# Output weights' parts stored once and loaded ready, and the attention's output split where it is copied, in a decoder-layer kernel

## The chip, the cores and the metric

The kernel runs on 1 core of a Trainium2 chip. The metric is device time in microseconds. The kernel before takes 3652.9 us (median of three runs, 3649.78 to 3656.28). The word core always means this one NeuronCore, with its engines TensorE (PE; its weight loads are PEld), VectorE (DVE), ScalarE (ACT), GpSimd (POOL) and SyncE (SP), which here issues nearly all DMAs.

## The reference, cut to what matters

One layer over 2048 prompt tokens and 64 sample tokens, model width 1024. An indexer picks 256 keys per token, eight heads attend to them (attention output `a_o`, 512 wide), and a state-space mixer gives `s_o` (512 wide). What follows is the part that the change touches:

```python
def residual_block(x, a_o, s_o, w_out, g_post, g_ffn_pre, w_up, w_down, g_ffn_post):
    mix = jnp.concatenate([a_o, s_o], axis=-1) @ w_out
    x = x + rmsnorm(mix, g_post)
    hdn = jnp.square(jax.nn.relu(rmsnorm(x, g_ffn_pre) @ w_up))
    return x + rmsnorm(hdn @ w_down, g_ffn_post)
```

## The kernel before, in words

The second half of the kernel (`blend`) starts at about 730 us. It walks a list of units, `plan`, and each engine executes its part of each unit in that one order. Units of three kinds are woven together by costs: the index search (`S`), the attention (`A`) and the feed (`W`, `M`, `N`, `U`, `D`, `E`), which is the residual block. The feed runs over four groups of 512 tokens (group 3 has a fifth tile, the samples). In a group:

- `W, g, h, i` is the output projection of token tile i into half h of the columns: 8 row blocks k of `w_out`, three matmuls each, 24 matmuls. All tiles of h = 0 come first, then all of h = 1.
- `M` is the norm after it and the norm before the MLP, tile by tile on ACT, DVE and POOL; `N` turns the result for the MLP.
- `U, g, j` (32 of them) and `D, g, m, q` (16 times four) are the MLP up and down; `E` is the last norm and the output store, beside the last `D` units and the next group's first `W` units.

Products are taken in three passes on operands split in two: hi (ACT rounds a copy to the reduced 32-bit format) and lo (DVE subtracts hi from the raw value). So a matrix needs one ACT copy and one DVE subtraction per piece before PE can use it. The MLP weights are split once, in group 0, stored to HBM in both parts (`ws_d`, L1343), and loaded ready by groups 1 to 3 into six slots (`load_ready`, L1339). The output weights are not: each group loads all 16 raw pieces (256 KB, L1352), ACT splits them (L1861) and DVE (L2197), into X, which holds one half h only. Half 0 of the next group is split beside the last eight `D` units, two pieces at each of four of them. Half 1 can only be split when the last `W, g, 0` unit has read X, at `W, g, 1, 0`.

The features of a tile are `a_d` (attention) and `so_d` (state space), 256 KB each, loaded by SP (L1365) and split by ACT (L1871) and DVE (L2204). Tiles 0 and 1 lie in region DN, 2 and 3 in H. PE waits for both low halves (L1574).

The attention's output of a tile is turned by PE (L1708) into one of two PSUM banks `tr`, copied by ACT (L1989), and stored by SP (L1463). The other uses of these banks are the turns of the probabilities (L1691), one per head and 512 keys.

SP has one queue of instructions and waits in order; a DMA whose wait is not yet met holds up all that stand behind it. `y_p` (L1428) is the store of the layer's result at `E`, which waits for POOL's last addition, and `m_d` (L1479) is the store of a selection mask, which waits for DVE's search.

## Time and profile before

| | |
|---|---|
| median of the runs | 3652.9 us (3649.78, 3652.9, 3656.28) |
| profiled execution | 3654.93 us, span 3653.3 us, mean granted clock 0.912 |
| PE busy | 3051.2 us, 84% |
| DVE, ACT, POOL busy | 1838.9, 1636.2, 1262.7 us |
| DMA | 529.45 MB, mean 145 GB/s |

Times are microseconds from the span's start, and the profiled execution's own time is its span and 1.6 us around it. PE is the busiest engine. Its longest idle stretches in the feed lie at the turns from one group to the next, at about 965 to 1078, 1623 to 1768, 2328 to 2475 and 3084 to 3209 us. In the rows, `x_hi_b` and `x_lo_b` are X, `dn_b` and `h_b` hold the features (and, elsewhere, `dn_b` down weights), `xs_b` is the raw input of the features, `r` are the three PSUM banks of the feed, `part_b` is where ACT copies a down sum from one of them before POOL adds it (L2111).

### The profile page before, as it was taken

The numbers are of one execution on the slowest core, as the hardware profiler recorded it, in microseconds if no ns is written. First come the engines' busy times: TensorE is split into PE (matmuls) and PEld (weight loads), VectorE is DVE, ScalarE is ACT, GpSimd is POOL, SyncE is SP. The second block draws the span as 40 slices with busy tenths as digits, with TensorE's granted clock in tenths as the row PEclk, the third lists the DMA queues.
The fourth block names the chain that finished last, engine by engine and source line by source line (L and its number), as shares of the span: only waits on it lengthen the run. The fifth ranks groups of instructions, "written<-read, shape, count | busy, mean of one in ns | idle before, by whom it ended". The sixth has DMA issues, their size and how long they took to land.

```text
span 3653.3 us, 46908 instructions
## 1 busy us (share of the span) xinstructions
PE 3051.2 (84%) x15352; PEld 2407.0 (66%) x15352; DVE 1838.9 (50%) x4116; ACT 1636.2 (45%) x2873; POOL 1262.7 (35%) x1181
## 2 busy tenths in 40 slices
PE   7998546557678889997799999869999999799997
PEld 6887432224566668765577886646778888578886
DVE  4333972862357974467785332666772333421112
ACT  3322413612456746575563456746734444322222
POOL 1333621323013551252264114522671112224444
PEclk9999767767889999997899999979999999899999
DMA  4444345636336573353454223343443213544443
GB/s 150 139 145 149 87 129 136 159 117 208 104 138 228 210 244 112 136 215 127 175 186 160 80 72 112 129 177 132 167 174 106 70 61 127 187 149 151 173 150 124
DMA packets 216109, 529.45 MB, mean 145 GB/s; under 512 B 57514, under 2 KB 110828, under 8 KB 189852
## 3 DMA queue, kind: packets, MB, share of 16 engines
q1 hardware_dynamic: 202924, 501.94, 40.4%
q0 software_dynamic: 11360, 22.60, 2.0%
q8 instruction: 125, 2.05, 0.2%
q10 hardware_dynamic: 1584, 1.90, 0.2%
q14 instruction: 116, 0.95, 0.1%
HBM read 399.43 MB, written 134.12 MB: 146 GB/s over the span
## 4 chain that ended last, share of the span: by engine, by line
PE 48%; DVE 12%; issue 11%; ACT 5%; DMA 4%; POOL 4%; SPq 2%; ACTq 0%; POOLq 0%; DVEq 0%
PE r L1620 16%; PE r L1652 12%; PE po L1700 4%; PE tr L1691 3%; ACT junk_a_b L1969 2%; POOL acc_b L2111 1%; PE sc L1679 1%; PE sc L1678 1%; PE r L1809 1%; PE sc L1668 1%; DVE junk_v_b L2350 1%; DVE trial_b L2302 1%; POOL hr_b L2092 1%; PE tr L1668 1%; DVE prob_b L2381 1%
## 5 line engine op out<-in xcount | busy, mean ns | idle before, releaser
L2111 POOL TENSOR_TENSOR acc_b<-acc_b,part_b 128x512 f32<-128x512 f32 x375 | 515.8, 1395 | 494.5 <-ACT part_b L1920 493.6
L1652 PE MATMUL r<-ready_b,h_b 128*128 128x512 f32 x2304 | 565.3, 401 | 44.2 <-ACT part_b L1920 40.2
L1652 PEld LDWEIGHTS r<-ready_b,h_b 128*128 128x128 f32 x2304 | 434.4, 192 | 159.7 <-ACT part_b L1920 52.4
L1620 PE MATMUL r<-x_hi_b,ready_b 128*128 128x512 f32 x1536 | 495.2, 396 | 5.4 <-DVE x_lo_b L2216 2.8
L2092 POOL TENSOR_TENSOR hr_b<-hr_b 128x512 f32<-128x512 f32 x128 | 148.8, 1163 | 780.9 <-ACT hr_b L1907 780.7
L1969 ACT ACTIVATE junk_a_b<-score_b,trial_b 128x384 int8<-128x384 f32 (+13 forms) x266 | 347.5, 1306 | 101.0 <-DVE trial_b L2302 99.9
L1620 PEld LDWEIGHTS r<-x_hi_b,ready_b 128*128 128x128 f32 x1536 | 292.0, 190 | 76.4 <-issue 10.1
L1920 ACT ACTIVATE part_b<-r 128x512 f32<-128x512 f32 x390 | 223.6, 594 | 216.6 <-PE r L1652 127.3
L1620 PE MATMUL r<-x_lo_b,ready_b 128*128 128x512 f32 x768 | 302.0, 393 | 0.0
L1700 PEld LDWEIGHTS po<-V_sb,pT_b 128*128 128x128 f32 x2176 | 286.1, 192 | 23.1 <-issue 3.1
L1996 ACT ACTIVATE pT_b<-tr 128x512 f32<-128x512 f32 (+3 forms) x320 | 168.7, 527 | 264.9 <-PE tr L1691 264.4
L1700 PE MATMUL po<-V_sb,pT_b 128*128 128x64 f32 x2176 | 279.0, 268 | 3.7 <-DVE o_b L2367 3.3
L2381 DVE CUSTOM_DVE_ANT_0 prob_b<-sc,mk_b,mx_b 128x512 f32<-128x512 f32 (+3 forms) x192 | 125.0, 651 | 286.8 <-PE sc L1679 286.4
L2350 DVE TENSOR_SCALAR_CACHE_REDUCE junk_v_b<-score_b,trial_b 128x384 bf16<-128x384 f32 (+13 forms) x182 | 268.2, 1474 | 1.8
L1652 PE MATMUL r<-dn_b,h_b 128*128 128x512 f32 x720 | 188.9, 417 | 42.3 <-ACT part_b L1920 21.0
L2100 POOL TENSOR_TENSOR h_b<-hr_b,h_b 128x512 fp32r<-128x512 f32 x128 | 185.8, 1452 | 96.4 <-ACT h_b L1936 96.4
L2381 DVE CUSTOM_DVE_ANT_0 prob_b<-sc,mk_b 128x512 f32<-128x512 f32 (+3 forms) x128 | 82.1, 642 | 246.3 <-PE sc L1679 177.7
L1691 PE MATMUL tr<-ident_sb,prob_b 128*128 128x128 f32 x1088 | 178.4, 280 | 31.1 <-ACT prob_b L2002 30.2
L1652 PEld LDWEIGHTS r<-dn_b,h_b 128*128 128x128 f32 x720 | 140.2, 200 | 89.3 <-ACT part_b L1920 26.1
L2002 ACT ACTIVATE prob_b<-prob_b,nmx_b 128x128 f32<-128x128 f32 (+15 forms) x128 | 153.9, 1202 | 99.9 <-DVE nmx_b L2387 99.9
L2293 DVE TENSOR_SCALAR turn_b<-count_b 128x1 int32<-128x1 f32 x448 | 68.2, 152 | 249.7 <-ACT junk_a_b L1969 240.4
L1907 ACT ACTIVATE hr_b<-r 128x512 f32<-128x512 f32 x128 | 75.6, 591 | 251.1 <-PE r L1620 251.1
(407 smaller groups left out, 6064.2 us busy)
## 6 DMA issues: line engine op xcount, KB each, us to landing
ready_b<-ws_u SPq DMA_DIRECT2D x96, 1024.0 KB, 6.6
ready_b<-ws_d SPq DMA_DIRECT2D x96, 1024.0 KB, 5.0
ws_u<-up_b SPq DMA_DIRECT2D x32, 1024.0 KB, 9.0
ws_d<-dn_b SPq DMA_DIRECT2D x30, 1024.0 KB, 6.5
kv_b<-kv_pages POOLq DMA_DIRECT2D x128, 128.0 KB, 3.4
kv_b<-kv_pages SPq DMA_DIRECT2D x128, 128.0 KB, 3.1
raw_b<-w_out SPq DMA_DIRECT2D x64, 256.0 KB, 3.4
raw_b<-w_up SPq DMA_DIRECT2D x32, 512.0 KB, 5.5
```

Source lines behind the costliest of these rows:

```text
L1620: mm = pe.matmul(x[:], wt[:, c], y[:, k], start=k == n == 0, stop=(k, n) == (KD - 1, 2))
L1652: mm = pe.matmul(x[:], f[:, tok], w[:, col], start=c == n == 0, stop=(c, n) == (KQ - 1, 2))
L1691: mm = pe.transpose(x[:, (k - 4 * b) * P:(k - 4 * b + 1) * P], prob[:, n % 2, k * P:(k + 1) * P], ident[:])
L1700: mm = pe.matmul(po[:, h, :], pT[:, prob_no[t, h, b] % 3, k - 4 * b, :], R["V"][:, k, n:n + HD], start=k == 0, stop=k == t)
L1920: act.activation(dst, ring[bank_no[key] % RING][:], ACT.Copy).then_inc(free_act, 1)
L1969: act.activation(junk_a[:, 0:width(t)], score[:, n % 3, 0:width(t)], ACT.Sign, bias=trial[:, 0:1].bitcast(F32), accum_out=count[:, 0:1]).t ...
L1996: act.activation(pT[:, j % 3, 0:m, :], tr[i % 2][:, 0:m * P].rearrange("p (k q) -> p k q", q=P), ACT.Copy).then_inc(tr_free, 1)
L2092: pool.tensor_tensor(s, s, s, ALU.mult).then_inc(sq_ok, 1)
L2100: pool.tensor_tensor(z, s, a.bitcast(F32), ALU.subtract).then_inc(h_lo_ok, 1)
L2111: pool.tensor_tensor(dst, dst, part[:, add_no[key] % 2, :], ALU.add).then_inc(add_pool, 1)
L2350: c.step(dve.tensor_scalar(junk_v[:, 0:width(t)], score[:, turn_s[t] % 3, 0:width(t)], trial[:, lower_trial(t)].bitcast(F32), 0.0, ALU.is_ ...
L2381: dve.tensor_tensor_reduce(out=prob[:, n % 2, 512 * b:512 * b + w], in0=sc[i % 2][:, 0:w], in1=mk[:, t % 2, 512 * b:512 * b + w], scale=1. ...
```

## The change

- Group 0 still loads and splits all 16 pieces. SP stores each split piece, both parts, to `wo_d` (16 stores of 512 KB). ACT's first split of half 1 waits for the eight stores of half 0, and its first `N` copy into X for all 16.
- Groups 1 to 3 load and split no raw piece. Half 0 is loaded into X by two DMAs of 2 MB once the previous group's last `U` has run. With it go the first three of eight row blocks of half 1, 1.5 MB in two DMAs, into free slot space (`kept_out`). The other five, 2.5 MB in one DMA, go into X once the last `W, g, 0` unit has run.
- For this slot space the fifth ready MLP piece of a group is loaded at the last `N` unit, beside the sixth, and not beside `W, g, 1, 3`.
- The attention's output is split where it is copied: ACT writes hi (still L1989's copy, now rounding), a new DVE instruction `low_output` writes lo from the same bank, and SP stores both (512 KB). PE waits for the low part before it uses that bank again. `aT` held two tiles; now it holds the two parts of one.
- A tile's attention features are loaded ready into place by one 512 KB DMA (`load_attended`), issued at the unit that uses them and not one tile ahead. Only `so_d` is split, with two input buffers. The sample tile is split as before.

```diff
@@ which parts are split, and where
-            at = [("D", g - 1, ND - 2, 2), ("D", g - 1, ND - 2, 3), ("D", g - 1, ND - 1, 0), ("D", g - 1, ND - 1, 1)]
-            for k in range(8):
-                splits_at[at[k // 2]].append(("wo", g, 0, k))
-        splits_at["W", g, 1, 0] += [("wo", g, 1, k) for k in range(8)]
         if g:
             continue
+        splits_at["W", g, 1, 0] += [("wo", g, 1, k) for k in range(8)]
...
-                where = ("W", g, 1, 3) if n == 4 else ("N", g, nt(g) - 1)
+                where = ("N", g, nt(g) - 1)
@@ memory
+    wo_d = nc.dram_tensor("wo_d", (2, P, 2, KD, 512), F32).ap()
+    a2_d = nc.dram_tensor("a2_d", (NPT, P, 2, 4, P), F32).ap()
+        KEPT = 3
+        kept_out = ready[:, 4:6].rearrange("p s z n -> p (s z) n")[:, 0:KEPT].rearrange("p k (z n) -> p z k n", z=2)
+        def out_weights(g, h, k):
+            if g and h and k < KEPT:
+                return kept_out[:, 0, k], kept_out[:, 1, k]
+            return X[0][:, k], X[1][:, k]
@@ SP
+                def keep_out(x):
+                    sp.wait_ge(lo_ok, split_no[x])
+                    sp.dma_start(wo_d[x[2], :, :, x[3]], x_both[:, :, x[3]].bitcast(F32)).then_inc(wo_st, 16)
+                def load_out(g, h):
+                    if h == 0:
+                        if g == 1:
+                            sp.wait_ge(wo_st, 16 * 16)
+                            sp.wait_ge(lo_ok, split_no["d", 0, NU - 1])
+                        sp.wait_ge(ring_full, all_up(g - 1, NU - 1))
+                        for n, k in enumerate((0, KD // 2)):
+                            sp.dma_start(x_both[:, :, k:k + KD // 2].bitcast(F32), wo_d[0, :, :, k:k + KD // 2]).then_inc(raw_ld[2 * n + 1], 16)
+                        for z in range(2):
+                            sp.dma_start(kept_out[:, z].bitcast(F32), wo_d[1, :, z, 0:KEPT]).then_inc(raw_ld[5], 16)
+                    else:
+                        sp.wait_ge(ring_full, full_at(("W", g, 0, nt(g) - 1)))
+                        sp.dma_start(x_both[:, :, KEPT:KD].bitcast(F32), wo_d[1, :, :, KEPT:KD]).then_inc(raw_ld[7], 16)
...
+                def load_attended(g, i):
+                    t, n = tile0(g) + i, feat_no[g, i]
+                    if i == 4:
+                        return
+                    sp.wait_ge(aT_st[t % 2], 16 * (t // 2 + 1))
...
+                    sp.dma_start(feat_both(i)[:, :, 0:4].bitcast(F32), a2_d[t]).then_inc(fa_ld[n % 2], 16)
...
                     for f, i in feats_at[u]:
+                        load_attended(f, i)
                         if i + 1 < nt(f):
                             load_features(f, i + 1)
+                    if kind == "D" and (u[2], u[3]) == (ND - 2, 2) and g + 1 < NG:
+                        load_out(g + 1, 0)
                     if kind == "W" and u[2:] == (1, 0):
+                        if g:
+                            load_out(g, 1)
@@ TensorE
-                        if i == 0:
+                        if i == 0 and g == 0:
                             pe.wait_ge(lo_ok, split_no["wo", g, h, k])
+                        elif i == 0 and h == 0 and k % 4 == 0:
+                            pe.wait_ge(raw_ld[2 * (k // 4) + 1], 32 + 16 * g)
+                        elif i == 0 and h and k in (0, KEPT):
+                            pe.wait_ge(raw_ld[7 if k else 5], 32 + (16 if k else 32) * g)
...
                     wait(pe, tr_free, n - 1)
+                    if n - 2 in output_at:
+                        pe.wait_ge(aT_lo_ok, output_at[n - 2] + 1)
@@ ScalarE, VectorE: features and the attention's output
-                    for k in range(2):
-                        act.wait_ge(f_ld[k], 16 * (n // 2 + 1))
-                        act.activation(feat(i)[0][:, 4 * k:4 * k + 4], f_in[:, k], ACT.Copy).then_inc(f_hi, 1)
+                    act.wait_ge(f_ld[n % 2], 16 * (n // 2 + 1))
+                    act.activation(feat(i)[0][:, 4:8], f_in[:, n % 2], ACT.Copy).then_inc(f_hi, 1)
...
+                def low_output(t):
+                    n = turn_no["o", t]
+                    dve.wait_ge(tr_free, n + 1)
+                    dve.tensor_tensor(aT[:, 1], tr[n % 2][:].rearrange("p (f q) -> p f q", q=P), aT[:, 0].bitcast(F32),
+                                      ALU.subtract).then_inc(aT_lo_ok, 1)
```

SP's queue at the start of group 0 (`raw_b` is a raw piece, `x_b` is X, `so_d` and `a_d` the two kinds of features, 1024 wide where both parts lie side by side). Before:

```order
L1352 DMA raw_b<-w_out 128x512 [waits y_st]
L1352 DMA raw_b<-w_out 128x512 x7
L1352 DMA raw_b<-w_out 128x512 [waits lo_ok_b] x8
L1365 DMA xs_b<-a_d 128x512 [waits aT_st0__b,h0_ld,bank_full]
L1365 DMA xs_b<-so_d 128x512
```

and after:

```order
L1364 DMA raw_b<-w_out 128x512 [waits y_st]
L1364 DMA raw_b<-w_out 128x512 x7
L1364 DMA raw_b<-w_out 128x512 [waits lo_ok_b] x8
L1343 DMA wo_d<-x_b 256x1x512 [waits lo_ok_b] x8
L1375 DMA xs_b<-so_d 128x512 [waits h0_ld,bank_full]
L1391 DMA dn_b<-a_d 128x2x512 [waits aT_st0__b]
```

Eight stores now stand between the raw loads and the first features.

SP's queue between groups 1 and 2, from the result's stores to the loads for the norm. Before:

```order
L1428 DMA y_p<-acc_b 128x1024 [waits y_ok_b] x4
L1365 DMA xs_b<-a_d 128x512 [waits f_lo_b,aT_st1__b]
L1365 DMA xs_b<-so_d 128x512 [waits f_lo_b]
L1479 DMA m_d<-tie_b 128x1664 [waits mask_ok_b]
L1399 DMA gbuf_b<-g_post 128x1024 [waits yn_ok_b]
L1375 DMA part_b<-x_all 128x1024 [waits add_pool_b]
```

and after:

```order
L1462 DMA y_p<-acc_b 128x1024 [waits y_ok_b] x4
L1391 DMA h_b<-a_d 128x2x512 [waits fa_ld0__b,ring_full_b,aT_st0__b]
L1375 DMA xs_b<-so_d 128x512 [waits f_lo_b]
L1391 DMA h_b<-a_d 128x2x512 [waits fa_ld1__b,ring_full_b,aT_st1__b]
L1513 DMA m_d<-tie_b 128x1664 [waits mask_ok_b]
L1357 DMA x_b<-wo_d 128x2x2560 [waits ring_full_b]
L1432 DMA gbuf_b<-g_post 128x1024 [waits yn_ok_b]
```

The attention features of tile 2 stood ahead of the `y_p` stores and now stand behind them, and the load of half 1's weights stands behind the mask's store.

DVE after the change, in the attention two steps behind a tile's turned output (ISA is the masked maximum over the scores in `sc`):

```order
L2439 ISA prob_b,mx_b<-sc,mk_b,mx_b 128x512 [waits sc_full_b,sc_free_b]
L2439 ISA mx_b 128x1
L2445 TENSOR_SCALAR nmx_b<-mx_b 128x1 [waits sc_free_b]
L2424 TENSOR_TENSOR aT_b<-tr,aT_b 128x512 [waits tr_free_b]
L2439 ISA prob_b,mx_b<-sc,mk_b 128x512 [waits sc_full_b,tr_full_b]
```

The TENSOR_TENSOR between them is new.

## Rows read from the trace of the kernel before

**Rows 1.** Page, busy time by engine.

```profile
PE 3051.2 (84%) x15352; PEld 2407.0 (66%) x15352; DVE 1838.9 (50%) x4116; ACT 1636.2 (45%) x2873; POOL 1262.7 (35%) x1181
```

**Rows 2.** PE, first matmul after its long waits (start, length, [idle <- releaser]).

```profile
984.46 0.80 PE L1586 MATMUL r<-x_hi_b,dn_b 128*128 128x512 f32 x1 [19.02 <-DVE dn_b L2204]
996.41 0.69 PE L1668 MATMUL sc<-kiT_sb,qi_b 64*128 64x512 f32 x1 [3.35 <-DMA qi_b<-qi_d]
1694.43 0.80 PE L1586 MATMUL r<-x_hi_b,h_b 128*128 128x512 f32 x1 [11.33 <-DVE h_b L2204]
1717.37 0.77 PE L1586 MATMUL r<-x_hi_b,dn_b 128*128 128x512 f32 x1 [5.71 <-DVE x_lo_b L2197]
2421.71 0.77 PE L1586 MATMUL r<-x_hi_b,dn_b 128*128 128x512 f32 x1 [9.04 <-DVE x_lo_b L2197]
3125.92 0.79 PE L1586 MATMUL r<-x_hi_b,h_b 128*128 128x512 f32 x1 [8.76 <-DVE h_b L2204]
3136.31 0.50 PE L1586 MATMUL r<-x_hi_b,h_b 128*128 128x512 f32 x1 [2.42 <-DVE h_b L2204]
3151.20 0.76 PE L1586 MATMUL r<-x_hi_b,dn_b 128*128 128x512 f32 x1 [2.02 <-DVE x_lo_b L2197]
```

**Rows 3.** Groups of instructions in 1635 to 1671 us, group 0's last down units.

```profile
L1652 PE MATMUL r<-up_b,h_b 128*128 128x512 f32 x48 | 16.8, 507 | 8.2 <-ACT part_b L1920 8.2
L2197 DVE TENSOR_TENSOR x_lo_b<-raw_b,x_hi_b 128x512 fp32r<-128x512 f32 x8 | 7.3, 955 | 0.4 <-DVE trial_b L2302 0.3
L2204 DVE TENSOR_TENSOR dn_b<-xs_b,dn_b 128x512 fp32r<-128x512 f32 x4 | 5.0, 1283 | 3.4 <-ACT dn_b L1871 3.4
```

**Rows 4.** Groups of instructions in 2331 to 2378 us, group 1's last down units.

```profile
L1652 PE MATMUL r<-ready_b,h_b 128*128 128x512 f32 x87 | 26.8, 462 | 12.0 <-ACT part_b L1920 12.0
L1969 ACT ACTIVATE junk_a_b<-score_b,trial_b 128x1792 int8<-128x1792 f32 x7 | 12.5, 1787 | 7.1 <-DVE trial_b L2302 7.1
L2197 DVE TENSOR_TENSOR x_lo_b<-raw_b,x_hi_b 128x512 fp32r<-128x512 f32 x8 | 8.3, 1089 | 0.1
```

**Rows 5.** Windows: busy us of PE, PEld, DVE, ACT, POOL; granted PE clock, DMA share, GB/s.

```profile
972.00:978.00 6.00, 0.00 (x0) 0.00 (x0) 4.14 (x7) 3.75 (x6) 0.00 (x0) 0.50 0.98 364
1735.00:1747.00 12.00, 6.10 (x27) 4.70 (x26) 6.11 (x15) 6.22 (x14) 3.16 (x2) 0.91 1.00 393
2331.00:2378.00 47.00, 35.02 (x103) 21.51 (x101) 41.82 (x65) 33.70 (x54) 22.31 (x16) 0.84 0.32 100
```

**Rows 6.** SP's queue at four places of the timeline.

```profile
978.07 0.37 SPq L1365 DMA_DIRECT2D xs_b<-a_d  x1
...
1693.85 0.33 SPq L1428 DMA_DIRECT2D y_p<-acc_b  x1
...
2420.87 0.32 SPq L1479 DMA_DIRECT2D m_d<-tie_b  x1
...
3130.44 0.33 SPq L1428 DMA_DIRECT2D y_p<-acc_b  x1
```

**Rows 7.** DMA issues: KB each, us to landing; at 1735.8 us, and at 1694.3 us.

```profile
x_d<-acc_b SPq DMA_DIRECT2D x1, 512.0 KB, 11.7
...
xs_b<-a_d SPq DMA_DIRECT2D x1, 256.0 KB, 3.2
```

**Rows 8.** Timeline, 1747 to 1749 us, group 1's norms.

```profile
1747.57 0.16 DVE L50 RECIPROCAL rs_b<-root_b 128x1 f32<-128x1 f32 x1 [4.38 <-DMA x_d<-acc_b]
...
1748.84 3.19 POOL L2126 TENSOR_TENSOR acc_b<-acc_b,part_b 128x1024 f32<-128x1024 f32 x1 [7.63 <-DMA part_b<-x_all]
```

**Rows 9.** Timeline, 1476 to 1485 us, behind the turned output of tile 6.

```profile
1476.07 0.61 PE L1708 MATMUL tr<-ident_sb,o_b 128*128 128x128 f32 x4
...
1478.26 0.61 PE L1691 MATMUL tr<-ident_sb,prob_b 128*128 128x128 f32 x4
...
1478.52 0.16 DVE L2387 TENSOR_SCALAR nmx_b<-mx_b 128x1 f32<-128x1 f32 x1
...
1481.78 2.99 PE L1652 MATMUL r<-dn_b,h_b 128*128 128x512 f32 x12
```

**Rows 10.** Line L2197 over the span: ns minimum/median/maximum.

```profile
L2197 DVE TENSOR_TENSOR x_lo_b<-raw_b,x_hi_b x64: 679/685/1792, 970.6 to 3154.6; 128x512 fp32r<-128x512 f32 x64
```

More of the change, by code:

```diff
@@ L922, in blend @@
     feats = [x for u in feed for x in feats_at[u]]
-    feat_no = {x: 2 * n for n, x in enumerate(feats)}
+    feat_no = {x: n for n, x in enumerate(feats)}
     def stream(g):
@@ L947, in blend @@
             holder[s] = x
-    for g in range(1, NG):
-        for k in range(8):
-            if g > 1:
-                behind_of["wo", g, 0, k] = 0
-                loads_at["U", g - 1, NU - 1 if k < 4 else NU - 1].append(("wo", g, 0, k))
-        for k in range(8):
-            behind_of["wo", g, 1, k] = split_no["wo", g, 0, k]
-            loads_at[at_split["wo", g, 0, k]].append(("wo", g, 1, k))
     WSLOTS = 6
@@ L1074, in blend @@
     head_at = {n: x for x, n in head_no.items()}
+    output_at = {turn_no["o", t]: t for t in range(NPT)}
     last_bank = lambda n: turn_no["p", *head_at[n], banks(head_at[n][0]) - 1]
@@ L1098, in place_at @@
             return t
-        X = [place_at(f"x_{n}", [P, KD, 512], F32R) for n in ("hi", "lo")]
+        x_both = place_at("x", [P, 2, KD, 512], F32R)
+        X = [x_both[:, n] for n in range(2)]
         H = place_at("h", [P, 8 * 512], F32R)
+        KEPT = 3
         ready = nc.alloc_sbuf_tensor_at("ready_b", [P, WSLOTS, 2, D], F32R, offset=at[0])
@@ L1211, in split_of @@
             if x[0] == "wo":
-                return X[0][:, x[3]], X[1][:, x[3]]
+                return out_weights(0, x[2], x[3])
             return piece(x)
@@ L1217, in split_after @@
             if kind == "wo":
-                if x[2]:
-                    return full_at(("W", g, 0, nt(g) - 1))
-                return all_up(g - 1, NU - 1) if g else 0
+                return full_at(("W", g, 0, nt(g) - 1)) if x[2] else 0
             c = x[2]
@@ L1235, in blend @@
         sring = [*sc, *tr]
-        raw_ld, wo_ld = [sem(f"raw_ld{i}_") for i in range(4)], [sem(f"wo_ld{i}_") for i in range(8)]
+        raw_ld = [sem(f"raw_ld{i}_") for i in range(8)]
         ready_ld = [sem(f"ready_ld{i}_") for i in range(WSLOTS)]
@@ L1355, in load @@
                             sp.wait_ge(xn_ok, last_tile(g))
[L1356 removed]
+                        sp.dma_start(raw_of(x), A["w_up" if kind == "u" else "w_down"][x[2]]).then_inc(raw_ld[2 * slot_of[x]], 16)
                 def load_features(g, i):
[L1359 to L1360 removed]
+                    t, n = tile0(g) + i, feat_no[g, i]
                     if i == 0:
                         wait(sp, res_ok, tile0(g))
[L1363 to L1365 removed]
+                    wait(sp, f_lo, n - 1)
+                    sp.dma_start(f_in[:, n % 2], A["so_d"][t]).then_inc(f_ld[n % 2], 16)
+                    if i == 4:
+                        sp.wait_ge(f_lo, n)
+                        sp.dma_start(f_in[:, 1 - n % 2], A["a_d"][t]).then_inc(f_ld[1 - n % 2], 16)
+                def load_attended(g, i):
+                    t, n = tile0(g) + i, feat_no[g, i]
+                    if i == 4:
+                        return
+                    sp.wait_ge(aT_st[t % 2], 16 * (t // 2 + 1))
+                    if g == 1 and i < 2:
+                        for z in range(2):
+                            sp.wait_ge(kept_st["DN", z], 16 * n_kept["DN", z])
+                    if g:
+                        sp.wait_ge(ring_full, all_down(g - 1, ND - 2 if i < 2 else ND - 1))
+                    wait(sp, fa_ld[n % 2], 16 * (n // 2))
+                    sp.dma_start(feat_both(i)[:, :, 0:4].bitcast(F32), a2_d[t]).then_inc(fa_ld[n % 2], 16)
                 def load_x(g, i):
@@ L1383, in feed_part @@
                     for x in splits_at[u]:
-                        if x[0] != "wo":
+                        if x[0] == "wo":
+                            keep_out(x)
+                        else:
                             keep(x)
@@ L1986, in keep_output @@
                     n = turn_no["o", t]
-                    wait(act, aT_st[t % 2], 16 * (t // 2))
+                    if t:
+                        act.wait_ge(aT_st[(t - 1) % 2], 16 * ((t - 1) // 2 + 1))
                     act.wait_ge(tr_full, n + 1)
-                    act.activation(aT[:, t % 2], tr[n % 2][:].rearrange("p (f q) -> p f q", q=P), ACT.Copy).then_inc(tr_free, 1)
+                    act.activation(aT[:, 0], tr[n % 2][:].rearrange("p (f q) -> p f q", q=P), ACT.Copy).then_inc(tr_free, 1)
                 def keep_prob(t, h, b):
```

71 lines of the change are left out of this document (39 added, 32 removed).

## The prediction

> **What bounds the kernel now.** I read the page first: PE is busy for 84% of the span [rows 1], no other engine for more than half. So the end is PE's stream of instructions, and DVE or ACT time taken away is worth what PE waited for it. Next I looked in PE's timeline for its waits around the output projection, where the removed work sits [rows 2]. There are two kinds: waits for a feature's low part (19.02, 11.33 and 8.76 us) and waits for the low part of half 1's first piece (5.71, 9.04 and 2.02 us). Then I grouped the instructions of the last down units of groups 0 and 1, where half 0 of the next group is split: PE waits there 8.2 and 12.0 us for ACT's copies `part_b` [rows 3, 4], at a mean granted clock of 0.84 in the second [rows 5], and DVE is busy for 41.82 of 47 us with the index search, the splits and the features. ACT's copies stand in its queue behind search counts, which wait for DVE's trial for 7.1 us there [rows 4]. Last I read SP's queue, which decides when the new loads start [rows 6], how long transfers took to land [rows 7], and who waited for them [rows 8]. Sums go against the profiled execution, 3654.9 us, which lies 2.0 above the median of 3652.9; the forecast is given against the median.
>
> **Group 0: 16 stores added.** Eight 512 KB stores, 4.2 MB, enter SP's queue just before the first features, where the load at 978.07 stood [rows 6]. At the 364 GB/s of the stretch before it [rows 5] they take 11.5 us. A 256 KB load landed after 3.2 us [rows 7], of which 0.7 is data at that rate, so 2.5 is fixed; of this I count 2 ahead of the data. The first features then follow at 978.1 + 2 + 11.5 + 0.7 = 992.3, their split (two operations near 0.7 each [rows 10]) ends at 993.7, and PE, which started at 984.46 [rows 2], is 9.2 late. It gets back the 3.35 us that it waited at 996.41 for the search's next load, which stood behind features that each waited for the split before them; with two buffers for `so_d` that load goes out sooner. The other eight stores stand ahead of the weights and tokens of the first norm, whose loads had several us to spare; I take 1.5. Sum +7.4. Bounds: +1 (the stores drain beside the raw loads) and +13 (nothing given back, 4 us at the norm).
>
> **Attention: the low part in front of the bank's next use.** Behind the turned output of tile 6, DVE's maximum and its small follower end at 1478.68; the new instruction takes 0.69 (a 512-wide subtraction [rows 10]) and ends at 1479.4. PE used the bank again at 1478.26 [rows 9]: +1.1 us. Twelve of 16 tiles have such a use soon behind them; where a unit of the feed stands in between (12 matmuls take 2.99 us [rows 9]) it costs nothing. I count seven at 1.1, less 1.7 for waits that follow and shrink: +6. Bounds 0 and +13 (12 at 1.1). Copy and stores cost nothing: ACT has one operation as before, and a doubled store has over 10 us before the next tile's copy waits for it.
>
> **Last down units before groups 1 and 2.** DVE loses eight `x_lo_b` (7.3 and 8.3 us) and half of the four feature subtractions (5.0, so 2.5 each time) [rows 3, 4]; ACT loses ten copies. Without the first, DVE has 41.8 - 10.8 = 31 us of work in 47 [rows 4, 5]. PE could get back at most its waits of 8.2 and 12.0 and what the clock took from it: at 0.84 over 35.02 busy us [rows 5] that is 5.6 us, so some 13 and 17 in all. The least is the 2.5 us of the features. Search and copies still wait for each other in turn, so I take a bit under two thirds: -8 and -11. Before group 3 no search is running, and I take 0.
>
> What the Trainium skill states bears on this: "SBUF — State Buffer", section "Who interferes with whom", says that a DVE instruction with two SBUF inputs and a GpSimd instruction that reads SBUF exclude each other, the second being blocked until the first ends. The trace agrees as far as it goes: `x_lo_b` has two SBUF inputs, and its mean beside POOL's additions is 955 and 1089 ns against a minimum of 679 [rows 3, 4, 10]. By that rule POOL's additions also come sooner once they are gone, which moves chance to the first rival.
>
> **Features of tile 2, groups 1 to 3.** The attention's half is now loaded behind the last `y_p` store. In group 1 that store went at 1693.85 [rows 6]; 0.4 us of issue and 3.9 for 512 KB (2.5 fixed, 1.4 data) put PE at 1698.1 instead of 1694.43, +3.7, less 1.7 since the chain to that store loses DVE work: +2. Group 2 is alike: +2. In group 3 the store went at 3130.44 while PE had started at 3125.92 [rows 2, 6]; by the order, the token loads ahead of it no longer wait for tile 1's split, so it should go 2 us sooner, and PE starts at 3132.7, +6.8. It gets back 2.42, the wait for tile 3 [rows 2], and about as much again because it runs on at the higher clock: +2. Together +6, bounds 0 and +14.
>
> **Half 1 of the weights.** Before, all 24 matmuls of a tile began after the wait. Now nine begin at once, and 15 when 2.6 MB have landed: 0.4 + 2.5 + 2.6 MB at 364 GB/s = 10.1 us after the last `W, g, 0`. The nine are worth 2.1 us (0.23 each at full clock, from 12 in 2.99 less the last one's tail [rows 9]). Group 1: 10.1 - 5.71 - 2.1 = +2.3. Group 3: 10.1 - 2.02 - 2.1 = +6.0. In group 2 the load stands behind the mask's store at 2420.87 [rows 6]: it lands at 2420.9 + 0.3 + 10.1 = 2431.3, against PE's start at 2421.71 [rows 2], so 9.6 - 2.1 = 7.5, less 3 for a search that is ahead: +4.5. Together +12.8, bounds +4 and +20. Behind SP's wait for the last `W, g, 0` stand the loads for the norm, which PE needs 20 us later; nothing there.
>
> **One MLP piece later.** The norm waits for the store of x (4.38 us) and POOL for a token load (7.63) [rows 8], both behind 5 MB of ready pieces: the store took 11.7 us to land [rows 7] at 393 GB/s [rows 5]. One MB less is 2.7 us in each of three groups: -8.1. Bounds 0 and -13 (three times 4.38).
>
> **Sum.** 7.4 + 6 - 19 + 6 + 12.8 - 8.1 = +5.1: profiled 3660, median 3658.
>
> **Rivals.**
> *The search was the whole brake.* The down units give back all, -13 and -17, and group 0's stores cost 3, not 7.4: 5.1 - 11 - 4.4 = -10.3, 3642.6. For it: DVE 41.82 of 47 busy, and the stretched subtractions. Against it: ACT's counts alternate with DVE's, whoever else is in the queue.
> *The loop keeps its pace (slower).* ACT copies `part_b` only behind a count that waits for DVE's trial, and splits only filled the pauses of that loop. Then the turns give back 2.5 each: 5.1 + 14 = +19, 3672. It decides when PE's waits for `part_b` stay above 6 us in each of the two turns.
> *The store burst is slow.* At half the rate the first eight take 23 us: +11.5, so +16.6, 3669.5. It decides when the stretch of the stores moves under 250 GB/s. Against it: 2 KB rows were loaded there at 364.
> *The change doesn't do what it says:* half 1 ready in time for all eight blocks would need the five blocks' load to start 8 us sooner, and X is not free then. I see no case for it; a smaller form, ready features that PE need not wait for, is the lower bound of two terms above.
>
> **Chances.** The forecast 0.40, with its own range 3649 to 3666; first rival 0.25, second 0.22, third 0.13. Under 0.2% (7.3 us) a measurement of this kernel can't tell a difference. Faster by more: most of the first rival and a twentieth of the forecast, 0.28. Slower by more (over 3660.2): the second, most of the third, and where the forecast's own range passes that line, 0.37. Within: 0.35. The range is 3637 to 3674.
>
> **What would show it.** In the profile after: PE's first projection matmul at 992 to 995 us, with the 3.35 us wait gone; a wait of about 1 us at the bank behind most turned outputs; PE's waits for `part_b` in the last down units at 2 to 5 us and DVE 9 to 11 us less busy there; PE's first `W, g, 0, 2` matmul bound by the load of `a_d` and not by DVE; in each of groups 1 to 3 a pause of 7 us or more after nine matmuls of half 1, longest in group 2; N's first turn about 3 us nearer to the last W. The forecast is wrong if group 0 costs under 3 us, or if the two turns together return under 10 or over 25.

## The result and the profile after

The changed kernel took 3685.3 us (median of 4 runs, 3682.9 to 3687.7) against 3652.9 for the kernel before on the same chip: ratio 1.0089, 95% interval 1.0071 to 1.0106. I had forecast 3658, with a range to 3674. Timed again later (e11) it took 3677.3 against 3656.1: ratio 1.0078, interval 1.0057 to 1.0098. So it is slower in both timings, by 21 and 32 us in the medians, not by 5. The page of the profiled execution (3687.1 us, span 3685.4) answers to [rows 1]:

```profile
PE 3039.1 (82%) x15347; PEld 2398.6 (65%) x15352; DVE 1803.9 (49%) x4068; ACT 1603.2 (44%) x2809; POOL 1258.5 (34%) x1181
```

DVE and ACT have 35 and 33 us less to do, PE has the same work and a span that is 32 us longer. PE's timeline shows where; these rows answer to [rows 2], in the same order of places:

```profile
998.71 1.62 PE L1628 MATMUL r<-x_b,dn_b 128*128 128x512 f32 x3 [31.08 <-DMA dn_b<-a_d]
...
1718.62 1.62 PE L1628 MATMUL r<-x_b,h_b 128*128 128x512 f32 x3 [15.71 <-issue]
...
1743.11 2.50 PE L1628 MATMUL r<-x_b,dn_b 128*128 128x512 f32 x5 [5.93 <-DMA x_b<-wo_d]
...
2419.70 2.90 PE L1628 MATMUL r<-x_b,h_b 128*128 128x512 f32 x6 [10.84 <-issue]
...
2448.60 1.65 PE L1628 MATMUL r<-x_b,dn_b 128*128 128x512 f32 x3 [12.80 <-DMA x_b<-wo_d]
...
3157.07 2.47 PE L1628 MATMUL r<-x_b,h_b 128*128 128x512 f32 x5 [15.11 <-issue]
...
3185.89 1.65 PE L1628 MATMUL r<-x_b,dn_b 128*128 128x512 f32 x3 [7.28 <-DMA x_b<-wo_d]
```

Every wait of [rows 2] that ended on DVE's splits now ends on a transfer or is gone ("issue" ends on one too: no instruction of another engine lies before it, and the ready half of tile 2 landed at 1718.53, 0.09 us ahead of PE's start). SP's queue, in the answer to [rows 6], says why. First group 0, then tile 2 of group 1, then half 1 of group 2:

```profile
980.87 9.38 SPq L1343 DMA_DIRECT2D wo_d<-x_b  x8
990.35 1.30 SPq L1375 DMA_DIRECT2D xs_b<-so_d  x1
991.69 1.21 SPq L1391 DMA_DIRECT2D dn_b<-a_d  x1
...
1702.63 11.35 SPq L1462 DMA_DIRECT2D y_p<-acc_b  x4
1714.10 0.53 SPq L1391 DMA_DIRECT2D h_b<-a_d  x1
...
2437.70 0.33 SPq L1513 DMA_DIRECT2D m_d<-tie_b  x1
2438.07 0.53 SPq L1357 DMA_DIRECT2D x_b<-wo_d  x1
```

To see how much of each length is the change and how much is the execution, I profiled both kernels again (e16, e8, e11) and cut each trace at the same instructions of PE: the turned outputs of tiles 4, 7, 8, 11, 12 and 15 (o4 ...), the first projection matmul of each group (W0 ...), and the last norm turn before each group's MLP (N0 ...). Lengths in us, each the difference of two starts in PE's timeline:

```
stretch      before  e16(before)  after   e8    e11    e1     e2     e10
o0  to o3      55.0     55.1      55.7   55.6   57.0   56.4   55.7   60.1
o3  to N0     110.2    108.7     119.3  118.6  117.8  127.7  102.9  109.2
N0  to o4     331.0    338.4     337.2  333.7  329.2  337.7  333.2  331.7
o4  to o7     101.9    101.9     104.9  104.8  104.9  101.9  104.9  102.0
o7  to W1     162.1    163.0     161.4  158.0  158.0  157.3  166.4  156.8
W1  to N1      95.3     95.7      97.4   98.3   97.9   94.4   99.4   88.3
N1  to o8     273.4    273.2     271.9  271.9  272.1  271.9  272.0  273.0
o8  to o11    159.9    159.9     162.6  162.6  162.6  159.9  162.2  161.5
o11 to W2     179.8    181.9     172.0  172.1  172.0  170.6  178.9  174.2
W2  to N2      93.5     91.8      98.6   98.8   98.4   98.3   93.4   82.5
N2  to o12    368.8    367.6     370.2  367.8  368.3  367.9  369.2  369.8
o12 to o15    221.0    221.0     224.3  224.3  224.4  221.0  224.0  221.0
o15 to W3      44.6     44.7      44.1   45.6   45.6   44.6   44.6   44.1
W3  to N3     100.4     99.9     107.3  105.3  107.6  103.7  103.3   97.9
```

Three things are to be seen. The last three attention stages differ by the same 2.7 to 3.4 us in every trace. The stages W to N are longer by 2.4, 6.0 and 6.6 (means of three traces against two). And N0 to o4, where both kernels do the same, varies by 7 and 8 us within either kernel. The rows of that stretch, of before, of e16, of after and of e11, have the same instructions and other clocks (0.94, 0.91, 0.91, 0.94):

```profile
1074.90:1405.90 331.00, 285.44 (x1202) 221.08 (x1203) 247.24 (x526) 200.74 (x350) 152.29 (x109) 0.94 0.61 215
```
```profile
1082.70:1421.20 338.50, 293.54 (x1203) 227.09 (x1204) 245.36 (x526) 201.17 (x350) 151.40 (x109) 0.91 0.59 210
```
```profile
1086.30:1423.50 337.20, 292.59 (x1202) 226.49 (x1203) 245.91 (x526) 201.06 (x350) 151.51 (x109) 0.91 0.60 211
```
```profile
1083.50:1412.70 329.20, 284.22 (x1202) 220.18 (x1203) 247.28 (x526) 200.79 (x350) 152.32 (x109) 0.94 0.61 216
```

The columns are those of [rows 5]. PE's busy time alone moves by 9 us, DVE's, ACT's and POOL's by 2 or less. So the pair of traces that I first laid side by side charged the change with 6 us here that belong to the execution.

### The profile page after: what moved, and what is told of

It is laid out like the page before. It is cut to its first block, busy times and chain, and to the rows that moved or that the text cites. A ratio compares the mean times of both kernels' runs of the same rounds, so it can differ in the third digit from the quotient of the medians.

```text
span 3685.4 us, 46737 instructions
## 1 busy us (share of the span) xinstructions
PE 3039.1 (82%) x15347; PEld 2398.6 (65%) x15352; DVE 1803.9 (49%) x4068; ACT 1603.2 (44%) x2809; POOL 1258.5 (34%) x1181
## 4 chain that ended last, share of the span: by engine, by line
PE 49%; DVE 11%; issue 10%; ACT 5%; DMA 4%; POOL 4%; SPq 2%; ACTq 0%; POOLq 0%; DVEq 0%
PE r L1662 16%; PE r L1694 12%; PE po L1744 4%; PE tr L1735 3%; ACT junk_a_b L2019 2%; POOL acc_b L2162 2%; PE r L1628 2%; PE sc L1721 1%; PE sc L1720 1%; PE sc L1710 1%; PE r L1853 1%; DVE prob_b L2439 1%; DVE junk_v_b L2402 1%; POOL hr_b L2143 1%; DVE trial_b L2354 1%
## 5 line engine op out<-in xcount | busy, mean ns | idle before, releaser
L1662 PE MATMUL r<-x_b,ready_b 128*128 128x512 f32 x2304 | 546.7, 395 | 5.4 <-DVE x_b L2268 2.8
L1662 PEld LDWEIGHTS r<-x_b,ready_b 128*128 128x128 f32 x2304 | 434.2, 190 | 105.6 <-issue 10.1
L2047 ACT ACTIVATE pT_b<-tr 128x512 f32<-128x512 f32 (+3 forms) x320 | 168.7, 527 | 274.0 <-PE tr L1735 273.6
L1662 PE MATMUL r<-x_b,up_b 128*128 128x512 f32 x768 | 187.4, 404 | 1.4 <-DVE x_b L2268 1.4
```

The costliest lines, as they stand in the source:

```text
L1662: mm = pe.matmul(x[:], wt[:, c], y[:, k], start=k == n == 0, stop=(k, n) == (KD - 1, 2))
L2047: act.activation(pT[:, j % 3, 0:m, :], tr[i % 2][:, 0:m * P].rearrange("p (k q) -> p k q", q=P), ACT.Copy).then_inc(tr_free, 1)
```

## The experiments

"Before" is the median of the kernel before, timed beside each version on the same chip. The expectations of e1 to e7 start from the first timing, 3685; e11 later put the changed kernel at 3677.3, and the gains below are smaller against that.

**e1, the stored weights alone.** Both feature halves raw and split as before, turned output copied once:

```
-    sp.wait_ge(aT_lo_ok, t + 1)
-    sp.dma_start(a2_d[t], aT[:].bitcast(F32))
+    sp.wait_ge(tr_free, turn_no["o", t] + 1)
+    sp.dma_start(A["a_d"][t], aT[:, t % 2])
```

> The changed kernel with the attention's part undone: one f32 copy per turned output, both feature halves loaded raw and split on ACT and DVE as before; the stored output weights stay. Comparing the two traces I put about 11 us of the 32 on the bank wait behind the turned outputs and 15 on tile 2's attended half behind the y_p stores. Theory A (those two sizes are right): 3685 - 11 - 15 + 5 for the splits that come back = 3664, and PE's wait ahead of tile 2 in groups 1 to 3 ends on DVE again, 5 us sooner. Rival B (the stored output weights are the dear part, the features only shift waits): 3675 to 3685. Rival C (the features were all of it): 3640 to 3650.

Measured 3671.7 against 3656.4, ratio 1.0044 (1.0027 to 1.0060). The place is as theory A had it (W1 to N1 94.4, the attention stages back at 101.9, 159.9 and 221.0), the time lies between A and B: o3 to N0 takes 127.7 us, 9 more than with both parts. There the features are raw again, and the search's load stands behind four of their splits as in [rows 2] (PE waits 4.74 us for it). Most of the rest is clock: from its first projection matmul to its last PE takes 69.8 us at a granted clock of 0.83, and 58.0 to 59.2 at 0.95 to 0.97 with both parts. Why the raw features bring the lower clock was not tried.

**e2, the attention's part alone,** on the kernel before.

> The kernel before with the attention's part alone: the low part made at the turned output, the attended half loaded as ready features; output weights raw and split as before. Theory A: 3653 + 11 + 15 - 5 = 3674. Rival B (stored weights are the dear part): 3653 to 3662. Rival C: 3680 to 3690. If A holds, e1 and e2 together lie 32 us above the kernel before twice over within 6 us.

Measured 3662.4, ratio 1.0017 (1.0005 to 1.0028): theory A's 3674 is refuted, B's range holds it. The bank wait is there (+3.0, +2.3, +3.0), but o3 to N0 is 6.6 us shorter than before: the search's load no longer waits in SP's queue behind four splits. Stretch by stretch e1 and e2 add up within 3.5 us: o3 to N0 +18.3 and -6.6 make +11.7 (after: +9.1), W3 to N3 +3.5 and +3.2 make +6.7 (after: +6.6), o11 to W2 -10.2 and -1.9 make -12.1 (after: -8.8).

**e3, the attended halves of tiles 2 and 3 ahead of the y_p stores:**

```
                 sp.dma_start(dst, x2_d[tile0(g) + i]).then_inc(x2_ld, 16)
+            if g + 1 < NG:
+                load_attended(g + 1, 2)
+                load_attended(g + 1, 3)
```

> The changed kernel with the attended halves of tiles 2 and 3 of groups 1 to 3 loaded behind the residual reload and ahead of the four y_p stores. Theory A: PE's waits ahead of tile 2 (15.71, 10.84 and 15.11 us) shrink by about 7, 5 and 5 and then end on DVE's split of the other half: 3685 - 17 = 3668. Rival D (the low clock and the next waits take it back: half 1's load starts when tile 3 ends, so the later pause is the same, and M's chain is bound by its own loads): 3678 to 3685.

Measured 3664.9, ratio 1.0021 (1.0011 to 1.0030): theory A. The loads go at 1683.63, 11 us ahead of the stores, and PE's wait in front of tile 2 ends on DVE:

```profile
1683.63 1.49 SPq L1391 DMA_DIRECT2D h_b<-a_d  x2
1694.70 11.38 SPq L1466 DMA_DIRECT2D y_p<-acc_b  x4
```
```profile
1703.55 8.01 PE L1632 MATMUL r<-x_b,h_b 128*128 128x512 f32 x24 [8.56 <-DVE h_b L2258]
...
2433.59 6.14 PE L1632 MATMUL r<-x_b,dn_b 128*128 128x512 f32 x15 [16.50 <-DMA x_b<-wo_d]
```

W1 to N1 falls from 97.9 to 91.3 and W3 to N3 from 106.7 to 100.3. In group 2 the stage falls only from 98.6 to 98.0: what tile 2 wins there PE waits for at half 1 (16.50 instead of 12.80).

**e4, the five late blocks apart:**

```
-    sp.dma_start(x_both[:, :, KEPT:KD].bitcast(F32), wo_d[1, :, :, KEPT:KD]).then_inc(raw_ld[7], 16)
+    for k in range(KEPT, KD):
+        sp.dma_start(x_both[:, :, k].bitcast(F32), wo_d[1, :, :, k]).then_inc(raw_ld[block_ld[k]], 16)
```

> The changed kernel with the five late blocks of half 1 loaded in five transfers of 512 KB, each with its own semaphore and waited for by the matmuls that read it. Theory A: block 3 lands about 5 us after its issue instead of 9 for all five, PE's pauses of 5.93, 12.80 and 7.28 us shrink by 3 each: 3685 - 9 = 3676. Rival D (what PE saves here it waits for in the norm behind it, whose loads stand behind the same blocks): no change, 3683 to 3686.

Measured 3676.7, ratio 1.0048 (1.0029 to 1.0067), 8.6 below the first timing of the changed kernel but at e11's level, and its six runs spread over 19 us: inconclusive as a time (its profile holds 5 us more in N1 to o8, at a granted clock of 0.95 instead of 0.98). The mechanism is in the trace: PE's pause in group 1 falls from 5.93 to 3.3 in five pieces (0.65, 1.53, 0.36, 0.38, 0.37), and the three stages W to N take 95.5, 94.4 and 104.0 instead of 97.9, 98.6 and 106.7, some 9 us in all.

**e5, group 0's stores later:** the first eight behind all features, the second eight behind the norm's loads.

```
-            keep_out(x)
+        if u == ("W", 0, 0, 1):
+            for k in range(KD):
+                keep_out(("wo", 0, 0, k))
...
```

> The changed kernel with group 0's stores moved: the first eight stand behind the loads of tiles 0 to 3's features and the search's load, the second eight behind the weights and the two token loads of the first norm. Theory A (the stores cost by what stands behind them in SP's queue): PE's first projection matmul returns from 998.7 to about 986, and the first norm turn from 1071 to about 1058, near where e2 had it: 3685 - 12 = 3673. Rival D (the stores still run beside half 1's split, which now waits for them on ACT, and beside M's loads; the gain is given back there): 3680 to 3688.

Measured 3668.4, ratio 1.0032 (1.0022 to 1.0043): theory A. PE starts at 987.37, o3 to N0 is 109.2, the length of before. ACT, which now waits for these stores before it splits half 1, cost nothing that shows; the norm is still later than before (26.3 us from the last projection matmul to N0, where before has 21.2), so the stores cost there wherever they stand, and what makes up for it is the shorter projection.

**e6, the bank freed by ACT alone:**

```
-    pe.wait_ge(aT_lo_ok, output_at[n - 2] + 1)
...
-    act.activation(aT[:, 0], tr[n % 2][:].rearrange(...), ACT.Copy).then_inc(tr_free, 1)
+    act.activation(o_turned, tr[n % 2][:], ACT.Copy).then_inc(tr_free, 1)
...
+    dve.tensor_copy(hi, o_turned).then_inc(aT_lo_ok, 1)
+    dve.tensor_tensor(lo, o_turned, hi.bitcast(F32), ALU.subtract).then_inc(aT_lo_ok, 1)
```

> The changed kernel with ACT copying the turned output to the (by then read) tile o in f32, as the bank's only reader; DVE then makes the high and the low part from that copy (one instruction more per tile), and PE no longer waits for DVE at the bank. Theory A: the 0.94 and following waits for aT go, each attention stage gets back about 2.5 to 3: 3685 - 10 = 3675. Rival E (DVE's extra instruction in the chain mask, maximum, exponential costs PE as much as the bank did): 3683 to 3690.

Measured 3682.3, ratio 1.0067 (1.0046 to 1.0088): the time is just under rival E's range and 7 us above theory A's, and against e11 nothing is gained. Three stages got back what theory A said (102.0, 161.5, 221.0). The first stage, with the samples' work beside it, became 3 us longer, with a new wait of 1.72 us for DVE, and the two turns o7 to W1 and o11 to W2 took 163.2 and 177.2 instead of 158.0 and 172.0.

**e7, e3 to e6 together.**

> e3, e4, e5 and e6 together. Their sum, if none overlap: 3685 - 20 (e3 as measured) - 9 (e4) - 12 (e5) - 10 (e6) = 3634. Overlap of e3 and e4 (a wait that shrinks twice) and clock that does not come back put it at 3640. Rival: the gains overlap down to the time of the kernel before, 3650 to 3656.

Measured 3643.3 against 3655.6, ratio 0.9967 (0.9956 to 0.9979): faster than both kernels, 9 short of the plain sum. That shortfall is no sign of overlap, since the sum starts from 3685: against e11's 3677.3 the medians of e3 to e6 alone come to 17 us less, and e7 is 34 less. By the stretches that they touch, e3, e4 and e5 alone are worth 13.6, 9.3 and 9.4 us, 32 together, and the three together (e9) 36. Group 2 shows what is left; PE was done with half 0 and with the nine ready matmuls of half 1 at 2407.7:

```profile
2414.20 0.33 SPq L1522 DMA_DIRECT2D m_d<-tie_b  x1
2414.57 3.33 SPq L1360 DMA_DIRECT2D x_b<-wo_d  x5
```
```profile
2419.68 3.94 PE L1641 MATMUL r<-x_b,dn_b 128*128 128x512 f32 x9 [11.97 <-DMA x_b<-wo_d]
```

**e8, the changed kernel once more,** unchanged.

> The changed kernel once more, as it is. In the comparison of before and after 7 us of the difference lie between the last norm turn of group 0 and the turned output of tile 4, and 6 between the outputs of tile 7 and the down units of group 0, with the same waits and a lower granted clock in both. Theory F (where the low clock falls is chance of the execution, so these 13 us are no cost of the change): this profile has them elsewhere or not at all, and the time lies between 3672 and 3688. Rival G (the clock follows the pauses, which are the same): the same stretches are slow again within 1 us each.

Measured 3673.2, one run. Theory F: N0 to o4 took 333.7 instead of 337.2, o7 to W1 158.0 instead of 161.4, and the stretches that the change does touch were the same within 1.6 us, W3 to N3 excepted (105.3 instead of 107.3).

**e9, e7 without e6.**

> e3, e4 and e5 together, without e6's copy to o. e6 alone left the time where it was within 3 us: it gave 3 back in three attention stages and lost 3.3 in the first and 5 in the last down units before group 2. Theory A (what e6 gained and lost cancels here too): 3643 to 3647, as e7. Rival E (e6 is worth its 10 once the rest is gone): 3653. Rival (e6's loss in the down units is the larger): 3638.

Measured 3644.1, ratio 0.9973 (0.9957 to 0.9989). e6 is worth nothing on top of the others, as theory A said.

**e10, half 1's load ahead of the search's steps:**

```
-    if g:
-        load_out(g, 1)          # at W,g,1,0
+    if kind == "W" and g and u[2:] == (0, nt(g) - 1):
+        load_out(g, 1)
```

> e7 with SP's load of half 1's late blocks ahead of the steps of the index search that stand between the last W,g,0 and the first W,g,1. In e7 PE waits 11.97 us for it in group 2, since it goes out at 2414.57 behind the mask's store (issued at 2414.20, when DVE has made the mask), while W,2,0 ended at 2407.70. Theory A: the load goes out at 2408 in group 2, half a us sooner in groups 1 and 3: 3643.3 - 6.5 = 3637. Rival D (M's chain behind it is bound by its own loads or by POOL, and takes the gain back): 3640 to 3645.

Measured 3631.0 against 3656.1, ratio 0.9943 (0.9926 to 0.9961): theory A, with 6 us more than it asked for. The load now goes 10 us ahead of the mask's store, and the long pause is gone:

```profile
2396.93 3.41 SPq L1360 DMA_DIRECT2D x_b<-wo_d  x5
2407.03 0.33 SPq L1522 DMA_DIRECT2D m_d<-tie_b  x1
```
```profile
2400.87 1.24 PE L1641 MATMUL r<-x_b,dn_b 128*128 128x512 f32 x3 [1.93 <-DMA x_b<-wo_d]
2403.38 1.65 PE L1641 MATMUL r<-x_b,dn_b 128*128 128x512 f32 x3 [1.26 <-DMA x_b<-wo_d]
2405.25 3.73 PE L1641 MATMUL r<-x_b,dn_b 128*128 128x512 f32 x9 [0.22 <-DMA x_b<-wo_d]
```

**e11, the changed kernel timed again.**

> The changed kernel once more, now timed against the kernel before in five rounds. The first timing put it 32.4 us above the kernel before (3685.3 against 3652.9), the single run e8 17.6 above the median of its own chip's runs of before. Theory F (the first timing had 10 us of low clock that the change does not bring with it): the median lies 18 to 25 us above before. Rival G (e8 was the outlier): 29 to 34 above.

The medians lie 21.2 us apart, which is theory F's; the ratio of 1.0078 with its interval says 21 to 36. That the first timing held some low clock that the change does not bring is likely, how much of the 32 it was stays open.

**e12, ACT's counts over half of each row.** What is left out: the upper 19 bits of each threshold are searched in half of the scores.

```
-    act.activation(junk_a[:, 0:width(t)], score[:, n % 3, 0:width(t)], ACT.Sign, ...
+    act.activation(junk_a[:, 0:width(t) // 2], score[:, n % 3, 0:width(t) // 2], ACT.Sign, ...
```

> The changed kernel with ACT's 266 counts of the index search over the first half of each row of scores instead of the whole (the threshold is halved with it; the choice of pages is then another one). Question: why the last down units before groups 1 and 2 gave back 6.7 and 7.0 us and not 8 and 11, with PE's waits for ACT's copies at 7.8 and 8.6 us there as against 8.2 and 12.0 before. Theory B (the loop of trial and count sets when ACT comes to the copies, whoever else was in the queues): with counts half as long those waits fall to 4 or less in each of the two turns, and the whole gets 10 or more us shorter from them: 3665 or less. Rival H (the copies are late because of POOL's sums or of the low clock, not of the counts): the waits stay at 7 or more.

Measured 3646.6, ratio 0.9980 (0.9965 to 0.9994). The whole is 31 us shorter than e11, but mostly in N0 to o4 and N2 to o12 (324.3 and 360.0, each 9 us less); the turns o7 to W1 and o11 to W2 give 3.5 and 4.2, and PE's waits for the copies in them are 6.9 and 6.9 us. Theory B's time is reached, but not where it said, and its waits of 4 or less are refuted. The three waits of group 1's turn hardly moved (1.68, 2.19 and 3.00 us, after: 1.67, 2.61 and 3.51), and the last one of group 2's turn, 5.38, not at all. ACT's queue in the changed kernel shows what stands ahead of that copy besides the count:

```profile
2381.78 1.79 ACT L2019 ACTIVATE junk_a_b<-score_b,trial_b 128x1792 int8<-128x1792 f32 x1 [2.12 <-DVE trial_b L2354]
...
2383.68 1.28 ACT L1930 ACT_TABLE_LOAD   x1
2385.28 0.20 ACT L1930 ACTIVATE root_b<-mean_b 128x1 f32<-128x1 f32 x1 [0.32 <-DVE mean_b L2294]
2385.42 1.06 ACT L1924 ACTIVATE hr_b<-acc_b 128x1024 f32<-128x1024 f32 x1
...
2386.48 1.06 ACT L1970 ACTIVATE part_b<-r 128x512 f32<-128x512 f32 x2
```

**e13, the last copies ahead of the norm on ACT:** root of tile 0 and square sum of tile 1 are put off behind the next unit's copies.

```
+    if before[u] is not None:
+        while late:
+            late.pop(0)()
...
-    square_root(u)
+    if put_off(u):
+        late.append(lambda: square_root(u))
+    else:
+        square_root(u)
...
```

> The changed kernel with one move on ACT: before groups 1 to 3 the last pair of copies part_b goes ahead of the square root of the closing norm's tile 0 and the square sum of its tile 1, behind which it stood. e12 halved the counts and PE's waits for the copies in the two last down units fell only from 7.8 and 8.6 us to 6.9 and 6.9, the last wait of group 2's turn (5.38) not at all: neither theory B nor the DVE work that I had blamed. Theory I (ACT's own queue ahead of the copy: a table load of 1.28 us, the root that waits for DVE's mean, the square sum of 1.06): the last wait of each turn (3.51 and 5.38) shrinks by about 2.5, 3677 - 5 to 3677 - 8, about 3670. Rival J (it is DVE's turn in that loop, and the norm's own chain then comes later and takes it back at the y_p stores and tile 2's features): 3675 to 3680.

Measured 3676.0 against 3657.0, ratio 1.0052 (1.0038 to 1.0066). The waits fall as theory I said, from 5.38 to 2.47:

```profile
2373.57 2.52 PE L1694 MATMUL r<-ready_b,h_b 128*128 128x512 f32 x6 [2.47 <-ACT part_b L1970]
```

and the turns with them (158.0 to 155.2, 172.0 to 168.7). The time is rival J's: W1 to N1 grows from 97.9 to 101.1, since the y_p stores wait for the norm that was put off and tile 2's half waits behind them: it goes out at 1701.83 instead of e11's 1700.19, although the first projection matmul comes at the same time in both (1675.5, 1675.6), and PE starts tile 2 at 1707.06 instead of 1704.65.

**e14, the same on e10.**

> e10 with the same move of ACT's last copies. In e10 tile 2's features no longer stand behind the closing norm, so what e13 wins in the turns should be kept: theory I 3631 - 7 = 3624; rival J 3629 to 3634.

Measured 3628.4, ratio 0.9924 (0.9908 to 0.9940), against e10's 0.9943 (0.9926 to 0.9961): the intervals overlap, so it is not shown to be better. The two are the fastest versions here.

**e15, e10 without the attention's part.**

> e10 without the attention's part: e1 (stored output weights, features raw) with group 0's stores later, half 1's blocks apart and its load sooner. Question: which part of the change pays once its costs are moved away. Theory K (the stored weights alone pay; the ready features only save two short instructions per tile): e1 3671.7 - 8.6 - 15 - 12 = 3636, within 5 us of e10. Rival L (the ready features matter, since tile 2's low part no longer waits for two splits on DVE): 3643 or more.

Measured 3642.6, ratio 0.9966 (0.9955 to 0.9977), about 12 us slower than e10: at rival L's edge. The two ratios' intervals just touch, but each of e15's 11 runs (3638.3 to 3652.1) is slower than each of e10's six (3624.8 to 3635.9). So the ready features pay once they are loaded in time. Half of it lies in group 0, where o3 to N0 takes 115.6 us instead of 109.2.

**e16, the kernel before once more.**

> The kernel before once more, for its profile: from the last norm turn of group 0 to tile 4's turned output it took 331.0 us, and 162.1 from tile 7's output to the first projection matmul of group 1, at a granted clock of 0.94; the changed kernel's first profile took 337.2 and 161.4 there, its second and third 333.7 and 157.9, and 329.2 and 158.0. Theory F (where the clock falls in the feed is chance): these lengths change by 2 to 6 us in the kernel before too. Rival G (before always has 331.0 and 162.1 within 1 us): then the spread belongs to the change.

3670.6 us in this run, with N0 to o4 at 338.4 instead of 331.0: theory F, in the kernel without the change. (o7 to W1 moved by 1 only.)

## Why the prediction was wrong, step by step

The new costs lay where I had put them: the stores ahead of the features, the bank, tile 2 behind y_p, half 1. The steps that failed are those that let time come back: the two thirds of the down units' waits, the give-back at tile 2, and, less, the count at the bank.

Measured sizes are means of the three traces of the changed kernel against the two of before, where nothing else is said.

- **Group 0's stores:** forecast +7.4, measured +9.1 (o3 to N0). That the two lie so near is luck: each of the three terms was too small, and the misses cancel. PE started 11.9 us later behind o3, not 9.2 (at 998.7, not 992 to 995, since the features landed in 6.7 us and not 3.2). From there to its last projection matmul it got back 10.5, not 3.35: the wait for the search's load went, and the same 224 matmuls ran at a granted clock of 0.97 instead of 0.83. First before, then after:

```profile
984.46:1053.80 69.34, 62.54 (x224) 46.65 (x224) 26.98 (x61) 34.29 (x71) 3.91 (x4) 0.83 0.40 136
```
```profile
998.71:1056.75 58.04, 54.24 (x224) 40.98 (x224) 20.44 (x47) 29.87 (x62) 0.58 (x2) 0.97 0.48 167
```

  That gain comes with the ready features (e2 has it: 61.5 us at 0.90; e1 does not: 69.8 at 0.83). And the norm cost 7.7, not 1.5: the second eight stores stand ahead of its loads, and POOL waited for a token load that took 9.7 us to land, where before it took 5.4 and POOL did not wait for it:

```profile
1069.95 3.18 POOL L2177 TENSOR_TENSOR acc_b<-acc_b,part_b 128x1024 f32<-128x1024 f32 x1 [5.86 <-DMA part_b<-x_all]
```

  The stores' stretch moved 376 GB/s, so the rival of the slow burst is refuted:

```profile
981.00:991.00 10.00, 0.00 (x0) 0.00 (x0) 0.00 (x0) 0.00 (x0) 0.00 (x0) 0.50 1.00 376
```

- **Bank wait behind the turned outputs:** forecast +6, measured +10.1 (1.0, 3.0, 2.7 and 3.4 in the four stages). The step that failed is the count of seven tiles and the 1.7 taken off for waits behind that would shrink. PE waits for aT nine times, 0.74 to 1.18 us each and 8.3 in all, near the 1.1 that I had for one. They are 2.3 to 2.6 us in each of the three later stages, and the stages are longer by at least that, so nothing came back. The first of them, behind tile 2:

```profile
958.51 0.63 PE L1735 MATMUL tr<-ident_sb,prob_b 128*128 128x128 f32 x4 [0.94 <-DVE aT_b L2424]
```

- **Last down units:** forecast -8, -11 and 0, measured -3.4, -8.8 and +0.4. With 7 us this is the largest miss. The stored weights alone bring more (e1: 157.3 and 170.6, that is -5.2 and -10.2); the attention's part alone lengthens o7 to W1 by 4 (e2). The step that failed is "Search and copies still wait for each other in turn, so I take a bit under two thirds": it has PE's waits for part_b fall to 2 to 5 us because DVE has less to do. They were 7.8 and 8.5, where [rows 3, 4] had 8.2 and 12.0. DVE's splits were not the brake, nor in the main were the counts (e12: 6.9 and 6.9 with counts half as long): half of the longest wait was ACT's own work for the closing norm (e13). What else holds the copies back stays open. What came back came in good part as clock: 0.98 and 0.89 in the stretches of the changed kernel, 0.84 in that of [rows 5] and 0.79 in the one before group 1. This is no chance of one execution: over the last 40 us before W1 the granted clock was 0.94 to 0.95 in the three traces of the changed kernel and 0.83 in both of before, and before W2 0.89 against 0.81 and 0.82. First the changed kernel's waits and windows, then that window of before:

```profile
L1694 PE MATMUL r<-up_b,h_b 128*128 128x512 f32 x48 | 13.1, 417 | 7.8 <-ACT part_b L1970 7.8
```
```profile
L1694 PE MATMUL r<-ready_b,h_b 128*128 128x512 f32 x89 | 23.7, 416 | 8.5 <-ACT part_b L1970 8.5
```
```profile
1655.00:1690.00 35.00, 27.09 (x97) 17.45 (x96) 28.77 (x56) 25.77 (x45) 18.60 (x15) 0.98 0.75 278
2353.00:2394.00 41.00, 32.46 (x106) 19.81 (x105) 34.22 (x59) 28.74 (x45) 21.30 (x16) 0.89 0.54 201
```
```profile
1635.00:1671.00 36.00, 27.67 (x78) 17.57 (x78) 31.42 (x59) 25.93 (x46) 17.28 (x12) 0.79 0.44 146
```

- **Tile 2 behind the y_p stores:** forecast +6, measured +11.6 (first traces, from the first W to the end of half 0: 3.3, 5.7 and 2.6). The mechanism and the gross delays held: +3.7 in groups 1 and 2 and +6.8 in group 3 by my working, +4.3, +4.7 and +6.4 measured (start of tile 2 after the first W). The step that failed is what I took off as given back, 1.7, 1.7 and 4.8. About 1 came back in group 1, nothing in group 2 (half 0 ended 5.7 later) and 3.8 in group 3; the y_p stores did not go sooner in groups 1 and 2. e3 shows the term by taking it away: 6.6, 0.6 and 6.4 us.
- **Half 1:** forecast +2.3, +4.5 and +6.0, measured +0.4, +3.2 and +5.8 on the first traces (from the end of half 0 to the end of half 1), +9.4 where I had 12.8. The step is right in groups 2 and 3 and 2 too high in group 1, where the load's pause was 5.93 us and not over 7. Tile 2's and half 1's terms lean on each other: in e3 tile 2 comes sooner in group 2, and PE waits for it at half 1. Both waits are real: e4 takes 9 us out of the three stages, e10 another 12 out of group 2's.
- **One MLP piece later:** forecast -2.7 in each group; from the last W to the first norm turn it was -1.6, -3.7 and -1.5 (first traces).
- **What no step had:** the feed of group 0 moves by 8 us with the clock in either kernel. A single profile of each cannot carry terms of that size there.

By the stretches this makes +9.1 + 10.1 - 3.4 - 8.8 + 0.4 + 15.0 (the three stages W to N) - 2.1 (N0 to o4, N1 to o8 and N2 to o12) = +20.3, close to e11's 21.2. (The profiled spans themselves differ by 15 only, because e16 took 9 us longer ahead of o0, where the change does nothing.) Against my +5.1 the misses are 7 in the down units, 4 in the attention, 4 in the stages W to N, 2 in group 0, and -2 that no step had. The rivals: the loop's pace had the criterion right (both waits above 6 us) and its time, 3672, was the nearest, but its cause is not shown: with counts half as long the waits fell by 0.9 and 1.6 us only. The rule of the Trainium skill ("SBUF — State Buffer", section "Who interferes with whom") does not decide here: POOL's additions in the two stretches went from 1460 to 1372 and from 1503 to 1407 ns once the two-input subtractions beside them were gone, which agrees with it, and PE's waits for part_b stayed at 7.8 and 8.5.

## What to carry to other kernels

Work that is taken off an engine and turned into a transfer is paid for in the queue that issues it: ask of each new load what stands ahead of it there, and put it where its buffer comes free, not where the old instruction stood. The same change was 0.8% slower as written and 0.6% faster (e10) when its loads and stores were moved and split in the queue, with the same matmuls on PE. (e10 also holds e6's change on ACT and DVE, which was worth nothing beside the others.) When working out such a sum, keep the gross delay, and take off only what a row shows to come back: at tile 2 I had 14.2 us gross, took off 8.2 as given back, and 11.6 came. In group 0 it went the other way, through the clock, which no row of before had shown me.
